# State-space stage of a hybrid backbone: order of subtractions, score rows, gate projections and PSUM banks

## Chip, core and metric

One core of one Trainium2 chip runs the whole program as one launch. The metric is the device time in microseconds (us), the median of several runs. TensorE is called PE here, VectorE DVE, ScalarE ACT, GpSimd POOL.

## What is computed

One layer on 256 context tokens and 512 latent tokens of width 1024: a modulated RMS norm, one input projection, three token mixers (gated linear attention, a 2-D Fourier mix, a bidirectional Mamba-2 state-space mixer), a gated merge, and a top-2 mixture of 16 experts. The change touches the state-space mixer alone, whose reference is, cut short:

```python
def ssd_chunked(x, dt, a, bm, cm, s0):
    '''h_t = exp(dt_t a) h_{t-1} + dt_t x_t B_t^T ; y_t = h_t C_t  (grouped B/C), chunked SSD.'''
    ...
    seg = a_cs[..., :, None] - a_cs[..., None, :]
    decay = jnp.exp(jnp.where(causal, seg, -jnp.inf))
    cb = jnp.einsum('bclgn,bcsgn->bcgls', cm, bm)
    y_diag = jnp.einsum('bcgls,bcgjls,bcsgjp->bclgjp', cb, decay, xdt)
    states = jnp.einsum('bcsgn,bcgjs,bcsgjp->bcgjpn', bm, decay_to_end, xdt)
    ...   # scan over chunks: s = chunk_decay * s + states
    y_off = jnp.einsum('bclgn,bcgjpn,bcgjl->bclgjp', cm, s_prev, jnp.exp(a_cs))
    y = (y_diag + y_off).reshape(B, T, H, P)
```

There are 4 groups of 8 heads of 64 channels, state size 128, and two directions. The result is gated: `rms_norm(y * silu(z)) @ proj`.

## The kernel before

Every engine has its own program, written out by hand in one fixed order, and the engines meet through semaphores only. All work is float32; a float32 matmul over 512 columns stands in the trace as two records. The kernel uses chunks of 128 tokens: 2 of context and 4 latent ones (`TC`, `TL`), taken in the order `ORDER[d]` by direction d.

**The state-space stage** is a loop over the groups g = 0..3. For one group PE does, in this order:

- `project_C` (L441): the C projection; then four x projections `("x", g, m)` (L441 for the latent and L445 for the context tokens, two PSUM banks each) with the transposes of B (L605), the score product CB (L614) and the transposes of x (`x_turn`, L420) between them.
- the z projections in pieces: `z_part(n)` (L629) issues the next n of the group's 32 matmuls, 8 to each of the four z tiles.
- the **first direction's state chain**: `first_state` (L667), then for i = 2..5 `state_step`, which is a state output ("off", four 128-column matmuls, L677) and, up to i = 4, a state part ("kv", one matmul, L684).
- the **loop of the first direction** (d = 0) over pairs of heads b = 0..3: `rows_of` for the next pair (L644 and L646, two matmuls a head, one bank a head, banks 0 and 1), the second direction's `first_state` (b = 0 only) and `state_step(1, b + 2)`, the pair's `y` product (L717, 16 records), and `z_part(2)`. The off and kv products of this direction share bank 2.
- the **loop of the second direction** (d = 1): rows of the next pair, y product of this one, pieces of the next group's B projection (`next_part`, L534; after the last group the first gate projection, L549) and the rows `spread` (L657) for its state outputs.

**The matrices of a head.** Head n of the stage has one of `NM = 4` buffers `mm`. DVE subtracts (`exponents`, L1855: PSUM rows minus a column), ACT takes the exponential (L1387), POOL multiplies by `cb` (L2321), and that allows the y product (`M_ready`). DVE may fill a buffer again once the y product that read it is over (`M_used`), so subtractions run at most two pairs ahead of the y products.

**The state chain.** DVE multiplies the off product out of its bank (L1827) and adds it to yT (L1831); it adds the kv product to the scaled state (L1839; a copy, L1836, for the first). An off product waits until DVE has read the kv before; a kv product waits until DVE has emptied bank 2 of the off product. POOL makes `xw` (L2283), the scaled state (L2303) and `xdt` (L2295). On DVE the second direction's `state_step` and the first direction's `exponents` stand in one hand-written sequence.

**ACT** has `z_silu(3)` (L1364), which needs the fourth z tile complete, between the exponentials of the two directions. Silu and Exp lie in different tables, so each change loads one.

**PSUM banks** are handed out while the program is built: `open_(pe, key, n, lo, hi)` takes the next n banks of the range lo..hi in rotation and makes PE wait until each earlier owner has been read. The x projections, the transposes and CB rotate through all eight banks. DVE's `finish` (L1865, L1872) empties the y banks 4 to 7, and ACT's `raw_evac` (L1286, L1287) empties the banks of B, C and x. Weights come in 2 MB strips through a ring of three slots on the SP queue.

Of the kernel before, what the change touches and what calls it, by code (L numbers as in the profile page):

```python
# [14 lines left out]
P = 128  # L15
D = 1024
T = 512
# [64 lines left out]
def build(nc, a, out):  # L82
    with ExitStack() as ctx:
# [310 lines left out]
        Z_STATES = (3, 3, 2, 2, 2)  # L394

# [15 lines left out]
        def x_turn(pe, g, m, lo=0):  # L411

            pe.wait_ge(S_("xc_ready"), g * 4 + m + 1)
            for half in range(2):
                key = ("xtok", g, m, half)
                ps = open_(pe, key, 1, lo, 8)
# [17 lines left out]
        def _(pe):  # L434
# [155 lines left out]
            for g in range(SG):  # L590
                if g:
                    project_C(g)

                slot = full_strip(pe, w_in, X0 + g * GW)
                for m in range(4):
                    project_T(slot, m, hT, ("x", g, m), nctx=True)
                    strip_used(("x", g, m))
                    if m == 0:
                        pe.wait_ge(S_("BT_ready"), g + 1)
                        for half in range(2):  # L600
                            key = ("Btok", g, half)
                            ps = open_(pe, key)
# [6 lines left out]
                    if m == 1:  # L609
                        pe.wait_ge(S_("CT_ready"), g + 1)  # L610
                        key = ("CB", g)
                        ps = open_(pe, key)
# [4 lines left out]
                    if m >= 1:  # L617
                        x_turn(pe, g, m - 1)
# [17 lines left out]
                x_turn(pe, g, 3, 4)  # L636
# [33 lines left out]
                def state_step(d, i, lo, hi):  # L670
# [9 lines left out]
                    if i < 5:  # L680
                        key = ("kv", g, d, i)
                        pe.wait_ge(S_("xw_ready"), (g * 2 + d) * 5 + i + 1)
                        ps = open_(pe, key, 1, lo, hi)
                        ins = mmul(ps[:, :], Btok[:, t, :], xw[i % 2][:, :], start=True, stop=True)  # L684
                        ins.then_inc(is_full(key)[0], 1)
# [3 lines left out]
                for i in range(2, 6):  # L689
                    for b in range(2):  # L690
                        if g == 0 or i >= 4:
                            spread(g, (i - 2) // 2, (i - 2) % 2 * 2 + b)
                    z_part(Z_STATES[i - 2])
                    state_step(0, i, 4, 8)
                z_part(Z_STATES[4])
                for d in range(2):
                    rows_of(d, 0)
                    rows_of(d, 1)
                    if d:
                        for i in range(2):  # L700
                            next_part(g + 1, i)
                    else:
                        yb = open_(pe, ("y", g), 4, 4, 8)
                    for b in range(HPG // 2):
                        n = (g * 2 + d) * HPG + 2 * b
# [7 lines left out]
                        pe.wait_ge(S_("xdt_ready"), (g * 2 + d) * 4 + b + 1)  # L713
                        pe.wait_ge(S_("M_ready"), n + 2)
                        for c in range(TL):
                            for h in range(2):
                                ins = mmul(yb[h * SHD:(h + 1) * SHD, b * T + c * P:b * T + (c + 1) * P],  # L717
                                           xdt[:, c, (2 * b + h) * SHD:(2 * b + h + 1) * SHD], mm[(n + h) % NM][:, c, :],
                                           start=(d == 0 and c == 0), stop=(d == 1 and c == TL - 1))
                        if d == 0 or b < 3:  # L720
                            ins.then_inc(S_("M_used"), 1)
                        else:
                            ins.then_inc(is_full(("y", g))[0], 1)
                        if d == 0:
                            z_part(2)
                            if b == 3:
                                strip_used(("z", g, 3))
                        else:
# [1734 lines left out]
```

## Time and profile before

| | |
|---|---|
| three runs | 1806.19, 1810.47, 1811.3 us; median 1810.47 us |
| the profiled execution | 1807.78 us, its span 1806.2 us |
| PE busy | 1633.8 us (90%), mean granted clock 0.967 |
| DVE, ACT, POOL busy | 665.0 (37%), 414.6 (23%), 282.8 us (16%) |
| state-space stage | about 90 to 700 us of the span |

A row of the chronological view gives the start, the duration, engine, line, operation, output and inputs, how many records were merged, and in brackets how long the engine stood idle before and which engine and line released it. The duration of a matmul runs to its modelled end, which is later than the start of the next one; the time that a matmul occupies PE is best read from one start to the next.

### The profile page before, as it was taken

The page shows a single profiled execution, that of the slowest core. Times are in us where ns is not written, and L with a number is a line of the kernel's source. Part 1 is how long each engine was busy: PE and PEld are TensorE (multiplying, and loading weights), DVE is VectorE, ACT ScalarE, POOL GpSimd, SP SyncE. Part 2 cuts the span into 40 slices and gives each one's busy share as a digit, 9 for nine tenths or more (in the row PEclk, how much of TensorE's full clock was granted, in tenths as well). Part 3 has the DMA queues.
Part 4 walks back from the last instruction along what each step waited for, and adds up shares of the span by engine and source line. Part 5 has one row for each costly group of instructions (what it writes and reads, how often), then busy time and mean ns, then how long its engine had stood idle before and what let it go on. Part 6 is the DMA issues. An engine that isn't in the chain of part 4 may idle for free. (4 is left out here: it accounts for less than half of the span.)

```text
span 1806.2 us, 23273 instructions
## 1 busy us (share of the span) xinstructions
PE 1633.8 (90%) x9106; PEld 875.3 (48%) x9107; DVE 665.0 (37%) x1086; ACT 414.6 (23%) x771; POOL 282.8 (16%) x311
## 2 busy tenths in 40 slices
PE   5998889899799899999999999999999949999893
PEld 2464454455455444444545555444656525555451
DVE  2544444354363455400126674214025122222224
ACT  4333423243242230000123324210120111111112
POOL 0006404503512530000000000000000022222122
PEclk9999999999999999999999999999989969999997
DMA  9810101101111056312110111123532467998994
GB/s 346 309 47 1 47 24 47 47 24 47 47 47 47 18 210 252 118 55 95 47 46 1 47 47 47 51 89 110 186 140 72 161 256 261 386 346 293 393 380 157
DMA packets 106754, 241.24 MB, mean 134 GB/s; under 512 B 5481, under 2 KB 15214, under 8 KB 106690
## 3 DMA queue, kind: packets, MB, share of 16 engines
q1 hardware_dynamic: 86800, 180.60, 27.8%
q0 software_dynamic: 14288, 48.96, 7.5%
q10 hardware_dynamic: 5602, 10.78, 1.6%
q8 instruction: 45, 0.74, 0.2%
q14 instruction: 19, 0.16, 0.0%
HBM read 218.31 MB, written 22.02 MB: 133 GB/s over the span
## 5 line engine op out<-in xcount | busy, mean ns | idle before, releaser
L441 PE MATMUL psum<-arena 128*128 128x512 f32 x688 | 303.5, 597 | 10.6 <-ACT arena L1287 5.7
L441 PEld LDWEIGHTS psum<-arena 128*128 128x128 f32 x688 | 129.0, 190 | 168.8 <-issue 162.9
L1083 PE MATMUL psum<-arena 128*32 128x256 f32 x2816 | 165.6, 387 | 1.5 <-DVE arena L2205 1.5
L455 PE MATMUL psum<-arena 128*128 128x512 f32 x352 | 155.5, 602 | 1.6 <-issue 1.6
L629 PE MATMUL psum<-arena 128*128 128x512 f32 x256 | 125.4, 626 | 1.0 <-ACT arena L1327 1.0
L1083 PEld LDWEIGHTS psum<-arena 128*32 128x32 f32 x2816 | 92.4, 111 | 59.7 <-issue 7.5
L772 PE MATMUL psum<-arena 128*128 128x512 f32 x256 | 111.5, 593 | 0.0
L455 PEld LDWEIGHTS psum<-arena 128*128 128x128 f32 x352 | 67.5, 194 | 84.0 <-issue 83.7
L2321 POOL TENSOR_TENSOR arena<-arena 128x512 f32<-128x512 f32 x64 | 85.9, 1353 | 98.2 <-ACT arena L1387 98.2
L1747 DVE SCALAR_TENSOR_TENSOR arena<-arena 128x772 f32<-128x772 f32 (+1 forms) x96 | 93.9, 978 | 3.4
L2283 POOL TENSOR_TENSOR arena<-arena 128x512 f32<-128x512 f32 x40 | 41.3, 1040 | 285.7 <-ACT arena L1327 280.7
L1105 PE MATMUL psum<-arena 128*32 128x256 f32 x1408 | 85.1, 382 | 1.0 <-DVE arena L2216 1.0
L2363 POOL DMA_DIRECT2D slots<-arena x92 | 50.1, 546 | 207.2 <-DVE arena L2216 179.7
L2337 POOL IOTA arena<- 128x4 int32 x1 | 0.1, 131 | 516.5 <-DVEq L408 516.5
L772 PEld LDWEIGHTS psum<-arena 128*128 128x128 f32 x256 | 47.9, 189 | 58.8 <-issue 58.8
L2210 DVE TENSOR_TENSOR arena<-arena,psum 128x128 f32<-128x128 f32 x44 | 12.7, 289 | 166.7 <-ACT arena L1587 166.7
L629 PEld LDWEIGHTS psum<-arena 128*128 128x128 f32 x256 | 47.2, 197 | 54.2 <-issue 54.2
L445 PE MATMUL psum<-arena 128*128 128x256 f32 x320 | 72.3, 378 | 0.0
L1855 DVE TENSOR_TENSOR arena<-psum,arena 128x512 f32<-128x512 f32 x64 | 42.6, 688 | 74.1 <-PE psum L646 73.0
L445 PEld LDWEIGHTS psum<-arena 128*128 128x128 f32 x320 | 60.4, 189 | 17.2 <-issue 9.6
L1387 ACT ACTIVATE arena<-arena 128x512 f32<-128x512 f32 x64 | 39.2, 629 | 109.7 <-DVE arena L1855 108.8
L717 PE MATMUL psum<-arena 128*64 128x128 f32 x512 | 38.8, 296 | 27.7 <-POOL arena L2321 27.7
(366 smaller groups left out, 2131.0 us busy)
## 6 DMA issues: line engine op xcount, KB each, us to landing
arena<-exp_w_d SPq DMA_DIRECT2D x48, 2048.0 KB, 17.4
arena<-w_in_d SPq DMA_DIRECT2D x22, 2048.0 KB, 8.0
arena<-ada_w_d POOLq DMA_DIRECT2D x8, 2048.0 KB, 10.4
slots<-arena POOLq DMA_DIRECT2D x1, 9216.0 KB, 27.0
arena<-ada_w_d SPq DMA_DIRECT2D x4, 2048.0 KB, 21.4
arena<-ssd_proj_d SPq DMA_DIRECT2D x4, 2048.0 KB, 11.3
slots<-arena POOLq DMA_DIRECT2D x92, 64.0 KB, 4.9
arena<-slots POOLq DMA_DIRECT2D x22, 256.0 KB, 6.0
```

The source lines that it names most:

```text
L441: ins = mmul(ps[:, 0:T], slot[:, k, m * P:(m + 1) * P], src[:, k, C:NT], start=(k == 0), stop=(k == KD - 1))
L445: ins = mmul(ps[:, T:T + C], slot[:, k, m * P:(m + 1) * P], src[:, k, 0:C], start=(k == 0), stop=(k == KD - 1))
L455: ins = mmul(ps[:, 0:n], src[:, k, t * P:(t + 1) * P], slot[:, k, 0:n], start=(k == 0), stop=(k == KD - 1))
L629: ins = mmul(bank(key)[:, :], slot[:, k, m * P:(m + 1) * P], hT[:, k, C:NT], start=(k == 0), stop=(k == KD - 1))
L772: ins = mmul(pss[m][:, :], slot[:, k, m * P:(m + 1) * P], yT[:, kh * KD + k, :], start=(kh == 0 and k == 0), stop=(kh == 1 and k == KD - 1))
L1083: ins = mmul(psU[q * R:(q + 1) * R, 0:2 * HF], XT[:, k % 2, k // 2, :], w13[p][:, :, k, q * HF:(q + 1) * HF], start=(k == 0), stop=(k == K ...
L1105: ins = mmul(psD[q * R:(q + 1) * R, 0:DQ], heT[:, k, :], w2[:, k, q * DQ:(q + 1) * DQ], start=(k == 0), stop=(k == NQ - 1))
L1747: ins = v.scalar_tensor_tensor(cacc[:, lo:hi], src[:, lo + k:hi + k], w[:, blk * SK + k:blk * SK + k + 1], cacc[:, lo:hi], ALU.mult, ALU.add)
L1855: v.tensor_tensor(mm[n % NM], bank(key)[:, :].rearrange("p (c l) -> p c l", c=TL), acs[:, TC:TT, at:at + 1].to_broadcast([P, TL, P]), ALU. ...
L2283: g_.tensor_tensor(heads(xw[i % 2]), heads(xtok[:, t, :]), wend[:, t, hs:hs + HPG].unsqueeze(2).to_broadcast([P, HPG, SHD]), ALU.mult).the ...
L2321: g_.tensor_tensor(mm[n % NM], mm[n % NM], cb, ALU.mult).then_inc(S_("M_ready"), 1)
L2363: pool.dma_start(rows(b)[:, q * DQ:(q + 1) * DQ].rearrange("(i r) c -> r i c", i=BATCH), half(ysb, b)[q * R:(q + 1) * R, :].rearrange("r ( ...
```

## The change

No operation is added or taken away. Four things change:

1. On DVE the first direction's `exponents` come in pairs: two of them, then one state step of the second direction. The first two subtractions of the second direction stand ahead of `state_step(1, 5)`.
2. On PE `rows_of` in the first loop still stands one pair ahead, and the last turn now issues the second direction's first pair (before, that came after the loop).
3. On PE the z matmuls of that loop leave their place behind the y product. One stands between `first_state` and the first off product, and 2, 2, 2 and 1 stand behind the off products, ahead of kv. POOL's `xw`, scaling and `xdt` are ordered by pairs to match.
4. From group 1 on, the x projections, the transposes and CB get fixed banks (`GROUP_BANKS`); group 0 keeps the rotation.

```diff
+        Z_BEHIND = (2, 2, 2, 1)
+        one = lambda *banks: tuple((b, b + 1) for b in banks)
+        ANY = (0, 8)
+        FIRST_BANKS = ([ANY] * 4, [(ANY, ANY)] * 3, (ANY, ANY), ANY)
+        GROUP_BANKS = (((4, 6), (6, 8), (3, 5), (5, 7)), (one(1, 2), one(7, 2), one(0, 1)), one(2, 3), (0, 1))
...
+                x_at, turn_at, btok_at, cb_at = GROUP_BANKS if g else FIRST_BANKS
...
-                    project_T(slot, m, hT, ("x", g, m), nctx=True)
+                    project_T(slot, m, hT, ("x", g, m), True, *x_at[m])
...
-                for d in range(2):
-                    rows_of(d, 0)
-                    rows_of(d, 1)
-                    if d:
-                        for i in range(2):
-                            next_part(g + 1, i)
...
-                    for b in range(HPG // 2):
-                        if b < 3:
-                            rows_of(d, 2 * b + 2)
-                            rows_of(d, 2 * b + 3)
-                        if d == 0:
-                            if b == 0:
-                                first_state(1, 2, 3)
-                            state_step(1, b + 2, 2, 3)
...
-                        if d == 0:
-                            z_part(2)
...
+                rows_of(0, 0)
+                rows_of(0, 1)
+                yb = open_(pe, ("y", g), 4, 4, 8)
...
+                for b in range(HPG // 2):
+                    for h in range(2):
+                        rows_of((b + 1) // 4, (2 * b + 2 + h) % HPG)
+                    if b == 0:
+                        first_state(1, 2, 3)
+                        z_part(1)
+                    state_off(1, b + 2, 2, 3)
+                    z_part(Z_BEHIND[b])
+                    if b < 3:
+                        state_kv(1, b + 2, 2, 3)
+                    else:
+                        strip_used(("z", g, 3))
+                    y_part(0, b)
+                for i in range(2):
+                    next_part(g + 1, i)
+                for b in range(HPG // 2):
+                    if b < 3:
+                        rows_of(1, 2 * b + 2)
+                        rows_of(1, 2 * b + 3)
+                    y_part(1, b)
...
@@ DVE
-                for i in range(1, 4):
-                    state_step(1, i)
-                    exponents(0, i + 1)
-                exponents(0, 5)
-                state_step(1, 4)
-                exponents(0, 6)
-                state_step(1, 5)
-                exponents(0, 7)
-                for h in range(4):
-                    exponents(1, h)
+                state_step(1, 1)
+                for i in range(2, 5):
+                    exponents(0, 2 * i - 2)
+                    exponents(0, 2 * i - 1)
+                    state_step(1, i)
+                exponents(1, 0)
+                exponents(1, 1)
+                state_step(1, 5)
+                exponents(1, 2)
+                exponents(1, 3)
@@ POOL
-                        if d == 0 and h in (1, 2, 4):
+                        if d == 0 and h in (1, 3, 5):
                             make_xw(1, 2 + h // 2)
-                        if d == 0 and h in (1, 3, 4):
                             scale_state(1, 2 + h // 2)
                         if d == 0 and h in (3, 5, 7):
                             make_xdt(1, h // 2 - 1)
-                        if d == 1 and h == 0:
+                        if d == 1 and h == 1:
                             make_xdt(1, 3)
```

How this moves the instructions, at three places. On **PE, the third and fourth turn of the first direction's loop in group 0**, before (L644 and L646 rows of a head, L677 off, L684 kv, L717 y, L629 z, L534 the next B):

```order
L646 MATMUL psum<-arena 128x512
L677 MATMUL psum<-arena 128x128 x4
L684 MATMUL psum<-arena 128x512
L717 MATMUL psum<-arena 64x128 x8
L629 MATMUL psum<-arena 128x512 x2
L677 MATMUL psum<-arena 128x128 x4
L717 MATMUL psum<-arena 64x128 x8
L629 MATMUL psum<-arena 128x512 x2
L644 MATMUL psum<-arena 128x512
```

and changed (L652 and L654 rows, L685 off, L694 kv, L719 y, L637 z, L541 the next B):

```order
L654 MATMUL psum<-arena 128x512
L685 MATMUL psum<-arena 128x128 x4
L637 MATMUL psum<-arena 128x512 x2
L694 MATMUL psum<-arena 128x512
L719 MATMUL psum<-arena 64x128 x8
L652 MATMUL psum<-arena 128x512
L654 MATMUL psum<-arena 128x512
L652 MATMUL psum<-arena 128x512
L654 MATMUL psum<-arena 128x512
L685 MATMUL psum<-arena 128x128 x4
L637 MATMUL psum<-arena 128x512
L719 MATMUL psum<-arena 64x128 x8
```

The z matmuls moved from behind y to between off and kv, and four row matmuls of the second direction stand in the last turn.

On **DVE, from the second direction's third state step on, group 1**, before (L1855 one subtraction, L1827 and L1831 the off product, L1839 kv):

```order
L1855 TENSOR_TENSOR arena<-psum,arena 128x512 x2
L1827 TENSOR_TENSOR arena<-psum,arena 128x512
L1831 TENSOR_TENSOR arena<-arena 128x4x128
L1839 TENSOR_TENSOR arena<-arena,psum 128x512
L1855 TENSOR_TENSOR arena<-psum,arena 128x512
L1827 TENSOR_TENSOR arena<-psum,arena 128x512
L1831 TENSOR_TENSOR arena<-arena 128x4x128
L1855 TENSOR_TENSOR arena<-psum,arena 128x512 x7
```

and changed (L1873 one subtraction, L1845 and L1849 off, L1857 kv):

```order
L1873 TENSOR_TENSOR arena<-psum,arena 128x512 x2
L1845 TENSOR_TENSOR arena<-psum,arena 128x512
L1849 TENSOR_TENSOR arena<-arena 128x4x128
L1857 TENSOR_TENSOR arena<-arena,psum 128x512
L1873 TENSOR_TENSOR arena<-psum,arena 128x512 x2
L1845 TENSOR_TENSOR arena<-psum,arena 128x512
L1849 TENSOR_TENSOR arena<-arena 128x4x128
L1873 TENSOR_TENSOR arena<-psum,arena 128x512 x4
```

Head 7's subtraction stood behind the last state step of the second direction; now heads 6 and 7 stand together ahead of the last but one, and the second direction's first two ahead of the last.

On **POOL, the products with `cb` of the first direction, group 1**, changed (L2339 a product, L2301 `xw`, L2321 the scaled state, L2313 `xdt`):

```order
L2339 TENSOR_TENSOR arena<-arena 128x512 x2
L2301 TENSOR_TENSOR arena<-arena 128x512
L2321 TENSOR_TENSOR arena<-arena 128x512
L2339 TENSOR_TENSOR arena<-arena 128x512 x2
L2301 TENSOR_TENSOR arena<-arena 128x512
L2321 TENSOR_TENSOR arena<-arena 128x512
L2313 TENSOR_TENSOR arena<-arena 128x4x128
L2339 TENSOR_TENSOR arena<-arena 128x512 x2
L2301 TENSOR_TENSOR arena<-arena 128x512
```

Two products now always stand together; before, other operations stood between the products of heads 2 and 3 and of heads 4 and 5.

## Rows read from the trace of the kernel before

**Rows 1.** PE's waits by line and releaser, 90 to 700 us: total us, times, longest

```profile
PE psum L717 <- POOL arena L2321: 27.7, 17, 4.3
PE psum L684 <- DVE arena L1827: 10.5, 12, 0.9
PE psum L441 <- ACT arena L1287: 5.7, 1, 5.7
PE psum L677 <- DVE arena L1836: 3.5, 4, 0.9
PE psum L644 <- DVE arena L1855: 2.4, 4, 0.6
...
PE psum L629 <- ACT arena L1327: 1.0, 1, 1.0
```

**Rows 2.** By stretch, groups 0 to 3: us, busy us by engine, clock, DMA share, GB/s

```profile
160.12:201.28 41.16, 31.55 (x156) 16.20 (x154) 17.76 (x25) 11.75 (x17) 23.43 (x20) 0.96 0.13 44
309.18:351.20 42.02, 32.42 (x156) 16.81 (x154) 17.77 (x25) 11.75 (x17) 23.42 (x20) 0.92 0.13 43
450.77:491.89 41.12, 31.52 (x155) 16.46 (x154) 17.78 (x25) 11.75 (x17) 23.43 (x20) 0.96 0.13 44
592.67:634.59 41.92, 30.61 (x151) 16.05 (x150) 17.79 (x25) 12.33 (x17) 23.56 (x21) 0.92 0.12 42
```

**Rows 3.** Chronological view, PE, group 1's first-direction loop: start us, duration us

```profile
302.35 1.05 PE L677 MATMUL psum<-arena 128*128 128x128 f32 x8
303.24 1.02 PE L684 MATMUL psum<-arena 128*128 128x512 f32 x2
...
316.45 1.10 PE L684 MATMUL psum<-arena 128*128 128x512 f32 x2 [0.88 <-DVE arena L1827]
317.48 1.10 PE L717 MATMUL psum<-arena 128*64 128x128 f32 x16
318.51 1.99 PE L629 MATMUL psum<-arena 128*128 128x512 f32 x4
320.33 0.38 PE L644 MATMUL psum<-arena 96*128 96x512 bf16 x1
...
321.21 1.05 PE L677 MATMUL psum<-arena 128*128 128x128 f32 x8
...
339.36 1.98 PE L717 MATMUL psum<-arena 128*64 128x128 f32 x16 [4.33 <-POOL arena L2321]
341.27 3.63 PE L629 MATMUL psum<-arena 128*128 128x512 f32 x4
```

**Rows 4.** The same view, DVE, same loop

```profile
329.71 1.81 DVE L1831 TENSOR_TENSOR arena<-arena 128x512 f32<-128x512 f32 x1
...
336.52 0.69 DVE L1855 TENSOR_TENSOR arena<-psum,arena 128x512 f32<-128x512 f32 x1
```

**Rows 5.** The same view, POOL, same loop

```profile
316.51 1.72 POOL L2321 TENSOR_TENSOR arena<-arena 128x512 f32<-128x512 f32 x1
318.19 1.04 POOL L2283 TENSOR_TENSOR arena<-arena 128x512 f32<-128x512 f32 x1
...
337.95 1.26 POOL L2321 TENSOR_TENSOR arena<-arena 128x512 f32<-128x512 f32 x1 [2.97 <-ACT arena L1387]
```

**Rows 6.** The same view, ACT, between the two directions

```profile
344.93 0.60 ACT L1364 ACTIVATE arena<-psum 128x512 f32<-128x512 f32 x1 [5.76 <-PE psum L629]
345.55 1.28 ACT L1387 ACT_TABLE_LOAD   x1
```

**Rows 7.** The same view, PE, from group 0 to group 1

```profile
217.74 7.13 PE L441 MATMUL psum<-arena 128*128 128x512 f32 x16
230.58 9.49 PE L441 MATMUL psum<-arena 128*128 128x512 f32 x16 [5.71 <-ACT arena L1287]
```

**Rows 8.** The same view, DVE, from group 0 to group 1

```profile
217.63 0.69 DVE L1865 TENSOR_TENSOR arena<-arena,psum 128x512 f32<-128x512 f32 x1 [0.74 <-PE psum L717]
```

**Rows 9.** The same view, PE, group 3's second direction

```profile
634.59 1.87 PE L717 MATMUL psum<-arena 128*64 128x128 f32 x16 [2.69 <-POOL arena L2321]
```

More of the change, by code:

```diff
@@ L415, in x_turn @@
                 key = ("xtok", g, m, half)
-                ps = open_(pe, key, 1, lo, 8)
+                ps = open_(pe, key, 1, *at[half])
                 for t in range(3):
@@ L601, in _ @@
                             key = ("Btok", g, half)
-                            ps = open_(pe, key)
+                            ps = open_(pe, key, 1, *btok_at[half])
                             for t in range(3):
@@ L611, in _ @@
                         key = ("CB", g)
-                        ps = open_(pe, key)
+                        ps = open_(pe, key, 1, *cb_at)
                         for c in range(TL):
@@ L635, in _ @@
                 z_part(Z_FRONT)
-                x_turn(pe, g, 3, 4)
+                x_turn(pe, g, 3, ((4, 8), (4, 8)))
                 pe.wait_ge(*is_free(("Btok", g, 1)))
@@ L679, in state_step, with state_kv @@
                     ins.then_inc(is_full(key)[0], 1)
[L680 to L685, printed above, removed]
+                def state_kv(d, i, lo, hi):
+                    key = ("kv", g, d, i)
+                    pe.wait_ge(S_("xw_ready"), (g * 2 + d) * 5 + i + 1)
+                    ps = open_(pe, key, 1, lo, hi)
+                    mmul(ps[:, :], Btok[:, ORDER[d][i], :], xw[i % 2][:, :], start=True, stop=True)\
+                        .then_inc(is_full(key)[0], 1)
                 z_part(2)
@@ L693, in _ @@
                     z_part(Z_STATES[i - 2])
[L694 removed]
+                    state_off(0, i, 4, 8)
+                    if i < 5:
+                        state_kv(0, i, 4, 8)
                 z_part(Z_STATES[4])
[L696 to L732 removed]
@@ new lines, in _, with y_part @@
+                rows_of(0, 0)
+                rows_of(0, 1)
+                yb = open_(pe, ("y", g), 4, 4, 8)
+                def y_part(d, b):
+                    n = (g * 2 + d) * HPG + 2 * b
+                    pe.wait_ge(S_("xdt_ready"), (g * 2 + d) * 4 + b + 1)
+                    pe.wait_ge(S_("M_ready"), n + 2)
+                    for c in range(TL):
+                        for h in range(2):
+                            ins = mmul(yb[h * SHD:(h + 1) * SHD, b * T + c * P:b * T + (c + 1) * P],
+                                       xdt[:, c, (2 * b + h) * SHD:(2 * b + h + 1) * SHD], mm[(n + h) % NM][:, c, :],
+                                       start=(d == 0 and c == 0), stop=(d == 1 and c == TL - 1))
+                    if d == 0 or b < 3:
+                        ins.then_inc(S_("M_used"), 1)
+                    else:
+                        ins.then_inc(is_full(("y", g))[0], 1)
@@ new lines, in _ @@
+                for b in range(HPG // 2):
+                    for h in range(2):
+                        rows_of((b + 1) // 4, (2 * b + 2 + h) % HPG)
[9 more added lines that the diff above has]
+                    y_part(0, b)
@@ L733, in _ @@
+                for i in range(2):
[5 more added lines that the diff above has]
+                    y_part(1, b)
+                    for i in range(2 * b + 2, min(2 * b + 4, 7)):
+                        next_part(g + 1, i)
+                    if g < SG - 1:
+                        spread(g + 1, 0, b)
             open_(pe, ("mod2",), 1, 7, 8)
```

10 lines of the change are left out of this document (3 added, 7 removed).

## Prediction

> **What bounds the kernel now.** The change touches one stage, so I read PE's waits there first [rows 1]. PE is the engine that nearly never stops, and what it waits for in this stage adds up to over 50 us. Half of it is one item: the y product waits 27.7 us in total for POOL's product L2321, 17 times, the longest 4.3 us. Next come 10.5 us in 12 equal waits of the kv product for DVE's L1827, one single wait of 5.7 us of an x projection, four waits of 0.9 us for the state copy L1836, four of 0.6 us for a subtraction, and 1.0 us once for ACT's L1327.
>
> Then the four stretches from a group's first row matmul to the first y product of the second direction [rows 2]. Each lasts 41 to 42 us, PE is busy for about 31, DVE for 18, ACT for 12, POOL for 23. No engine is full: the stretch is bound by latency, by who waits for whom. The clock column says more: 0.92 to 0.96, so part of PE's busy time is at the lower level.
>
> The chronological view shows where [rows 3]. The last y product of the first direction stands idle for 4.33 us, and after that the same 16 records take 1.98 instead of 1.10 us and the z matmuls 3.63 instead of 1.99: half speed, 1.2 instead of 2.4 GHz. Who is late? POOL's product starts at 337.95 after ACT, ACT after DVE's subtraction at 336.52 [rows 4, 5]. That subtraction is head 7's, and in DVE's order it stands behind the second direction's last state step, which needs the off product that PE issues only in this turn. So PE issues the off product, and the y product right behind it must wait for a chain DVE, ACT, POOL that begins with the off product. That is the 4.33 us, once in each of four groups. Afterwards ACT needs Silu on the fourth z tile (0.60 us), whose matmuls stand behind this late y product, and a table load (1.28 us), before it can take the second direction's first exponentials [rows 6]; this gives another wait for POOL at the end of each stretch.
>
> **The change, part by part.** I count PE's work in one stretch from start to start, which is the time a step takes from PE, at full clock [rows 3]: one pair of heads' rows 0.88 us (320.33 to 321.21), off 0.89 (302.35 to 303.24), kv with the change to y 1.03 (316.45 to 317.48), y 1.03 (317.48 to 318.51), two z matmuls 1.82 (318.51 to 320.33). The stretch holds six pairs of rows (5.3), `first_state` as two kv (1.8), four off (3.6), three kv (3.1), four y (4.1), eight z (7.3) and four full B matmuls at a kv's 0.88 (3.5): 28.7 us. No part of the change alters this sum.
>
> *z between off and kv.* It covers the time in which DVE empties bank 2 (0.69 us and the way there and back) with 1.8 us of matmuls. The 12 waits of 0.88 us go, and one z matmul of 0.9 us covers the copy behind `first_state` all but 0.1 us. What z covered so far was the way to the next y product. That cover is needed only if the matrices come late, and this is what the pairs are for.
>
> *Subtractions in pairs.* I walk through the new order, t = 0 at the stretch's start. PE: first rows, the 0.6 us wait for the bank stays, second rows until 2.5; `first_state` to 4.3; z, off, two z, kv to 9.0; y(0) to 10.0. A turn is now 0.9 + 0.9 + 1.8 + 1.0 + 1.0 = 5.7 us: y(1) ends at 15.7, y(2) at 21.4. The last turn has rows, off and one z: y(3) starts at 24.1. The other engines: DVE subtracts heads 4 and 5 at 10.7, as soon as y(0) has freed their buffers and the rows are there, ACT follows within 1.4 us, POOL's two products need 2.5 us. POOL must do `xw`, the scaling and an `xdt` in each turn besides: 2 x 1.26 + 3 x 1.04 = 5.6 us [rows 5], just under PE's 5.7. In this order POOL ends the products of heads 4 and 5 at 15.4 (needed at 20.4) and those of heads 6 and 7 at 21.1 (needed at 24.1). Nothing waits for M before the last y product, and 3.0 us are to spare there. The 4.33 us go, and with them the half clock.
>
> *The second direction's start.* Its rows and subtractions are now early. What is late next is Silu: the fourth z tile is full at 24.1; Silu, the table, two exponentials and two products give 0.6 + 1.3 + 0.7 + 2.6 and hand-overs, 29.4. PE has y(3), the B matmuls and one pair of rows and arrives at 29.6. So the wait is gone where four B matmuls stand there (groups 0 to 2). In group 3 only two gate matmuls stand there, PE arrives at 27.9 and waits 1.6 us: 29.5.
>
> Sum of the stretches: 41.16 + 42.02 + 41.12 + 41.92 = 166.2 us before [rows 2], 3 x 29.6 + 29.5 = 118.3 after: **47.9 us**. In group 3 there is a second wait of 2.69 us, inside the stretch, and the y product behind it takes 1.87 instead of 1.10 us [rows 9]; with the projection that follows I put 1.6 us for the slow clock there.
>
> *Fixed banks.* The 5.7 us wait stands at the passage from group 0 to 1: the rotation gave the first x projection bank 1, in which the C projection lies that PE has just made, and ACT empties it only after B's convolution. x starts at 230.58 instead of 224.6 (217.74 and eight times 0.86), and its eight matmuls take 9.49 instead of 7.13 us [rows 7]: **8.3 us**. With the fixed banks it lies in 4 and 5, whose owner is y. DVE's last read of y starts at 217.63 and takes 0.69 us [rows 8], 6.3 us before x needs the bank. The 1.0 us wait of a z product for ACT's L1327 is a wait for a bank too (group 3); its new owner is an older transpose. **1.0 us**.
>
> What stays: about 1 us in each group at the last y product (what is left of the 27.7 us) and the 0.6 us above. The later stages wait for nothing that has a time of its own; all start from this stage's end, so they move as a whole.
>
> Does faster work collide? A DVE sum of two SBUF operands takes 1.81 us where another operation of this size takes 0.69, and a POOL product 1.72 instead of 1.26, where the two run together [rows 4, 5]. By the largest of each, POOL's products cost 8 x 0.46 = 3.7 us more in a stretch; 3.0 are to spare, so 0.7 us a group would show. I take none in the sum, since most products in these rows stand at 1.26. The Trainium skill says why the two meet (GPSIMD Engine Reference, Key points: the engine shares its SBUF interfaces with VectorE, with contention when VectorE reads two SBUF inputs). By that rule packing POOL fuller makes it slower, and the sum would be that of the first rival; the trace agrees as far as these two rows go.
>
> Total: 47.9 + 1.6 + 8.3 + 1.0 = 58.8 us. Against the profiled execution's 1807.8 us this gives 1749.0. Its time is 2.7 us under the median of the three runs, so for a median I say **1750**.
>
> **The rivals.**
> - *POOL becomes the bound of the first loop.* If all its operations stretch by 1.72 / 1.26, a turn takes 7.6 us against PE's 5.7. Over three turns 6 us are lost, 3 of them are spare: 3 us a group, 12 in all, 1762. For it: POOL is busy without a gap from 3 to 21 in my walk. Against: 23 us busy in 42 now, with few long ones. At the middle of the way it costs 6 us, 1756. Chance 0.12.
> - *The fixed banks move the wait instead of removing it*, to a transpose or a z product that now meets a younger owner. Then 8.3 us stay or stand in three passages at 2 to 3 us each: 1758. Against: each new owner that I followed is read microseconds before. Chance 0.05.
> - *The change does not do what it says.* If DVE still gets to heads 6 and 7 late, because a subtraction waits for a y product that waits for POOL, the 4.33 us and the slow clock stay (4 x 6.4 us): 1776. The order of the instructions speaks against it. Chance 0.03.
> - *Slower.* From group 1 on x always needs banks 4 to 7, which y holds until DVE's last step. If that step came later than the 6.3 us after y's end, PE would stand, with the clock loss of [rows 7] (2.4 us) on top. Only if it came some 26 us late would three passages at 22 us eat the gain and more: 1815. DVE has 18 of 42 us to do here, and its step follows y within 1 us. Chance 0.02.
>
> **How the numbers follow.** The forecast has 0.78. Its own bounds: the steps are read to 0.1 us, 16 turns, and the remaining waits of a few us, 1743 to 1756. The range must take in the first two rivals to their upper prices: 1743 to 1763. A measurement of this kernel tells 0.3% (5.4 us) from no change. Faster by more 0.97, within it 0.01, slower 0.02.
>
> **What would show it.** PE's waits for POOL fall from 27.7 us to 4 to 7, with no wait over 2 us. The waits of kv for DVE and the 5.7 us are gone. The four stretches last 29 to 30 us at clock 1.00. Wrong would be: a y product in the first loop that waits for POOL (POOL as the bound), a new wait behind an x projection (banks), or a stretch of the later stages that grew.

## The result, and the profile after

The changed kernel takes 1741.41 us, the median of 4 runs (1738.72 to 1744.89), against 1809.85 us before: ratio 0.962, 95% interval 0.961 to 0.964. Faster was forecast, 1750 us with a range from 1743 to 1763: the gain is 68 us where 60 were forecast, and the time lies 1.6 us below the range. The profiled execution took 1743.69 us (span 1742.1), 64.1 us less than the one profiled before.

The page of the changed kernel, PE's busy time and the granted clock in 40 slices:

```profile
PE 1613.3 (93%) x9106; PEld 865.1 (50%) x9107; DVE 663.0 (38%) x1086; ACT 414.4 (24%) x771; POOL 284.2 (16%) x311
...
PEclk9999999999999999999999999999999969999997
```

and the same clock line of the kernel before:

```profile
PEclk9999999999999999999999999999989969999997
```

PE is busy for 1613 us, 20 us less than before with the same work. Most of that is time at half clock that is gone: by the mean granted clock PE lost 59.6 us of its span to the lower level before (0.033 of 1806.2) and 43.6 now (0.025 of 1742.1), 16 us less. The page's 40 slices are too coarse to show where: both lines stand at 9 all through this stage, though [rows 2] has 0.92 to 0.96 there. The short stretches below show it.

PE's waits by line and releaser from 90 to 700 us (total, times, longest), to be laid beside [rows 1]:

```profile
PE psum L719 <- POOL arena L2339: 5.4, 6, 1.5
PE psum L652 <- DVE arena L1873: 2.4, 4, 0.6
PE psum L675 <- POOL arena L2301: 1.4, 4, 0.4
PE psum L652 <- ACT arena L1391: 0.9, 6, 0.2
PE psum L448 <- DVE arena L1883: 0.8, 1, 0.8
PE psum L685 <- DVE arena L1857: 0.6, 1, 0.6
```

L719 is the y product: 5.4 us in 6 waits instead of 27.7 in 17. The 12 waits of kv, the copy's four, the 5.7 us at the x projection and the 1.0 us of a z product are not there. The row waits (L652) are those of before.

The four stretches from the first row matmul of a group to the second direction's first y product, by stretch, to be laid beside [rows 2]:

```profile
161.51:190.70 29.19, 28.56 (x155) 15.16 (x154) 15.89 (x24) 11.03 (x15) 23.14 (x20) 1.00 0.15 51
290.27:319.45 29.18, 28.56 (x155) 15.16 (x154) 15.94 (x24) 11.02 (x15) 23.13 (x20) 1.00 0.15 51
419.00:448.21 29.21, 28.59 (x156) 15.16 (x154) 16.86 (x24) 11.03 (x15) 23.06 (x20) 1.00 0.15 51
547.78:576.78 29.00, 26.91 (x151) 14.43 (x150) 16.95 (x25) 12.12 (x17) 22.96 (x20) 1.00 0.15 49
```

29.2, 29.2, 29.2 and 29.0 us instead of 41.2, 42.0, 41.1 and 41.9, all at clock 1.00. PE is busy for 28.6 of them.

Group 1's loop on PE in the chronological view (L652 a row, L685 off, L637 z, L694 kv, L719 y, L541 the next group's B), to be laid beside [rows 3]:

```profile
300.21 0.39 PE L652 MATMUL psum<-arena 96*128 96x512 bf16 x1
...
301.10 1.05 PE L685 MATMUL psum<-arena 128*128 128x128 f32 x8
301.99 1.88 PE L637 MATMUL psum<-arena 128*128 128x512 f32 x4
303.71 1.02 PE L694 MATMUL psum<-arena 128*128 128x512 f32 x2
304.66 1.10 PE L719 MATMUL psum<-arena 128*64 128x128 f32 x16
305.70 0.39 PE L652 MATMUL psum<-arena 96*128 96x512 bf16 x1
...
313.91 1.10 PE L719 MATMUL psum<-arena 128*64 128x128 f32 x16
314.94 3.70 PE L541 MATMUL psum<-arena 128*128 128x512 f32 x8
...
319.45 1.10 PE L719 MATMUL psum<-arena 128*64 128x128 f32 x16
```

No bracket stands in these rows: none of these instructions waited. A turn takes 5.49 us (300.21 to 305.70). The last y product of the direction (313.91) and the first of the next (319.45) come when PE gets to them; before, the first of these two stood idle for 4.33 us. POOL in the same loop (L2339 products, L2313 `xdt`):

```profile
303.53 2.95 POOL L2339 TENSOR_TENSOR arena<-arena 128x512 f32<-128x512 f32 x2
...
308.45 1.55 POOL L2313 TENSOR_TENSOR arena<-arena 128x512 f32<-128x512 f32 x1
309.96 2.50 POOL L2339 TENSOR_TENSOR arena<-arena 128x512 f32<-128x512 f32 x2
```

The products of heads 6 and 7 end at 312.5, the y product needs them at 313.9: 1.5 us to spare, not 3.0. A pair of products takes 2.95 us and one `xdt` 1.55 where DVE's sum of two SBUF operands (L1849) stands beside them, and 2.50 and 1.04 elsewhere in this loop:

```profile
302.92 1.20 DVE L1849 TENSOR_TENSOR arena<-arena 128x512 f32<-128x512 f32 x1
...
308.40 0.69 DVE L1849 TENSOR_TENSOR arena<-arena 128x512 f32<-128x512 f32 x1
```

The passage from group 0 to 1 (C projection and x projection merged into one row), beside [rows 7]:

```profile
207.16 14.00 PE L448 MATMUL psum<-arena 128*128 128x512 f32 x32
```

16 matmuls (32 records) in 14.0 us without a wait, 0.87 us each, the pace of the first row of [rows 7].

**Where the 64 us came from.** Cut at the first row matmul and at the first matmul behind the state-space stage (both starts from the chronological view):

| | up to the first row | state-space loop | later stages |
|---|---|---|---|
| before | 160.1 | 489.8 | 1156.2 |
| changed | 161.5 | 429.0 | 1151.6 |
| difference | +1.4 | -60.8 | -4.7 |

The stage gave 60.8 us where 58.8 were forecast. The later stages, which the change does not touch in the code, gave 4.7 us where nothing was. The experiments are about both. The 1.4 us lost ahead of the first row are clock: from 30 us of the span to the first row PE does the same work, and is busy for 126.2 us at a mean granted clock of 0.95 instead of 124.6 at 0.96. Why was not tested.

### The profile page after: what moved, and what is told of

Read it like the earlier page. It is cut to its first block and busy times, and to the rows that moved or that the text cites. A ratio compares the mean times of both kernels' runs of the same rounds, so it can differ in the third digit from the quotient of the medians.

```text
span 1742.1 us, 23271 instructions
## 1 busy us (share of the span) xinstructions
PE 1613.3 (93%) x9106; PEld 865.1 (50%) x9107; DVE 663.0 (38%) x1086; ACT 414.4 (24%) x771; POOL 284.2 (16%) x311
## 5 line engine op out<-in xcount | busy, mean ns | idle before, releaser
L448 PE MATMUL psum<-arena 128*128 128x512 f32 x688 | 300.9, 593 | 3.6 <-DVEq L415 2.8
L448 PEld LDWEIGHTS psum<-arena 128*128 128x128 f32 x688 | 128.1, 189 | 160.1 <-issue 154.2
L462 PE MATMUL psum<-arena 128*128 128x512 f32 x352 | 154.1, 597 | 0.0
L1101 PEld LDWEIGHTS psum<-arena 128*32 128x32 f32 x2816 | 91.9, 111 | 60.8 <-issue 7.9
L637 PE MATMUL psum<-arena 128*128 128x512 f32 x256 | 118.8, 596 | 0.0
L790 PE MATMUL psum<-arena 128*128 128x512 f32 x256 | 111.5, 593 | 0.0
L2339 POOL TENSOR_TENSOR arena<-arena 128x512 f32<-128x512 f32 x64 | 87.6, 1389 | 45.4 <-ACT arena L1405 45.4
L2301 POOL TENSOR_TENSOR arena<-arena 128x512 f32<-128x512 f32 x40 | 41.3, 1040 | 277.8 <-ACT arena L1345 272.8
L790 PEld LDWEIGHTS psum<-arena 128*128 128x128 f32 x256 | 47.9, 189 | 58.8 <-issue 58.8
L637 PEld LDWEIGHTS psum<-arena 128*128 128x128 f32 x256 | 45.4, 189 | 47.4 <-issue 47.4
L1873 DVE TENSOR_TENSOR arena<-psum,arena 128x512 f32<-128x512 f32 x64 | 41.8, 688 | 52.9 <-PE psum L654 52.4
L837 PE MATMUL psum<-arena 128*128 128x512 f32 x128 | 61.1, 595 | 0.0
L905 PE MATMUL psum<-arena 128*128 128x512 f32 x128 | 57.0, 607 | 2.1 <-ACT arena L1507 2.1
```

What stands on the lines that cost most here:

```text
L448: ins = mmul(ps[:, 0:T], slot[:, k, m * P:(m + 1) * P], src[:, k, C:NT], start=(k == 0), stop=(k == KD - 1))
L462: ins = mmul(ps[:, 0:n], src[:, k, t * P:(t + 1) * P], slot[:, k, 0:n], start=(k == 0), stop=(k == KD - 1))
L637: ins = mmul(bank(key)[:, :], slot[:, k, m * P:(m + 1) * P], hT[:, k, C:NT], start=(k == 0), stop=(k == KD - 1))
L790: ins = mmul(pss[m][:, :], slot[:, k, m * P:(m + 1) * P], yT[:, kh * KD + k, :], start=(kh == 0 and k == 0), stop=(kh == 1 and k == KD - 1))
L837: ins = mmul(bank(key)[:, :], slot[:, k, key[1] % 4 * P:(key[1] % 4 + 1) * P], hT[:, k, C:NT], start=(k == 0), stop=(k == KD - 1))
L905: ins = mmul(ps[:, :], slot[:, k, m * P:(m + 1) * P], src[:, k, :], start=(k == 0), stop=(k == KD - 1))
```

## The experiments

For every kernel the same two lengths are given, "stage" and "later", from its one trace; the times are medians of several runs. The kernel before was run again beside each set. Theory A is my forecast's: a part is worth the waits it removes and the slow clock behind them.

### Each part alone or left out

**Fixed banks alone**, in the kernel before, from group 1 on; `x_turn`, `Btok` and `CB` get theirs likewise:

```diff
-                    project_T(slot, m, hT, ("x", g, m), nctx=True)
+                    project_T(slot, m, hT, ("x", g, m), True, *x_at[m])
...
```

> The kernel before with the fixed banks alone, all orders as before. Theory A (each part is worth the waits it removes): the 5.7 us wait of the first x projection of group 1, the slow clock behind it (2.4 us) and the 1.0 us z wait go, everything else stays: 9 us faster than before, about 1801, with the y products' 27.7 us of waits for POOL unchanged. Rival B (the parts need each other; the wait only moves while the loop is slow): 0 to 3 us faster, with a new wait behind an x projection or a transpose. Rival C (the later stages gained because the state-space stage ends earlier): a part of the later stages' gain shows here too, from the end of this stage on over 2 us.

Measured: 1792.6 us against 1809.4, ratio 0.992 (0.990 to 0.995). Stage 480.5 (-9.4), later 1149.7 (-6.6). PE's waits from 90 to 700 us:

```profile
PE psum L723 <- POOL arena L2327: 27.6, 17, 4.3
PE psum L690 <- DVE arena L1833: 10.5, 12, 0.9
```

The y products wait 27.6 us as before, the x projection does not wait. For the stage theory A holds to 0.4 us, and B falls. But the kernel is 17 us faster, not 9: the rest lies in the later stages. C had the place right; the reason is another, as the rotation below shows.

**The changed kernel without fixed banks:**

```diff
-                x_at, turn_at, btok_at, cb_at = GROUP_BANKS if g else FIRST_BANKS
+                x_at, turn_at, btok_at, cb_at = FIRST_BANKS
```

> The changed kernel with the rotation of banks as before. Theory A: 9 us slower than the changed kernel, about 1750, by one wait of 5 to 6 us at the first x projection of group 1 with a stretch of half clock behind it. Rival B: within 2 us of the changed kernel, since the C projection's bank is emptied in time when the group ends earlier.

Measured: 1755.2 us (1748.9 to 1760.8), ratio to before 0.970 (0.967 to 0.972). Stage 438.5, 9.5 more than the changed kernel; later 1159.4, 7.8 more.

```profile
PE psum L448 <- ACT arena L1305: 5.7, 1, 5.7
PE psum L719 <- POOL arena L2339: 5.4, 6, 1.5
...
PE psum L637 <- ACT arena L1345: 1.0, 1, 1.0
```

The 5.7 and the 1.0 us are back to the digit. B falls: ending the group earlier doesn't help, since C's bank is late relative to C. In all it is 14 us slower than the changed kernel where 9 were expected; the stage gives the 9.5, the rest stands in the later stages. The six times stand in two groups, three from 1748.9 to 1750.7 at a mean clock of 0.975 to 0.977 and three from 1759.8 to 1760.8 at 0.970 or 0.971: the same program, 10 us (0.6%) apart, as its clocks are. The trace, and with it the 1159.4, is of the slowest of the six.

**z between off and kv alone**, in the kernel before (`state_step` takes the number of z matmuls to issue behind its off product):

```diff
                                 first_state(1, 2, 3)
+                                z_part(1)
-                            state_step(1, b + 2, 2, 3)
+                            state_step(1, b + 2, 2, 3, (2, 2, 2, 1)[b])
...
-                        if d == 0:
-                            z_part(2)
```

> The kernel before with the z products between off and kv alone (1, then 2, 2, 2, 1), subtractions and rows as before. Theory A: the 12 waits of kv and most of the 4 for the state copy go (13 us, 17 with the hand-over), the wait at the last y product falls by one z matmul to about 3.4 us, the 1 us wait at the second direction's first y goes since Silu comes earlier, and a new wait of about 1 us stands at the third y: some 20 to 28 us faster than before, about 1786. Rival B (without the pairs the z products are missed behind y, and the waits for POOL grow by what kv no longer waits): under 10 us faster, over 1800, with the waits for POOL above 35 us.

Measured: 1784.9 us against 1809.4, ratio 0.987 (0.985 to 0.989). Stage 467.9 (-21.9), later 1156.6, as before.

```profile
PE psum L721 <- POOL arena L2321: 23.2, 15, 3.5
PE psum L441 <- ACT arena L1287: 5.7, 1, 5.7
PE psum L644 <- DVE arena L1855: 4.6, 8, 0.6
```

A holds: 24.5 us faster, and kv no longer waits. The y products' waits fall only from 27.7 to 23.2, the longest is 3.5 (one z matmul stands ahead of it now), and the x projection's wait is untouched. The rows' waits for DVE grow from 2.4 to 4.6 us, which was not expected.

**The pairs without z**: the changed kernel with z behind y:

```diff
                         first_state(1, 2, 3)
-                        z_part(1)
                     state_off(1, b + 2, 2, 3)
-                    z_part(Z_BEHIND[b])
...
                     y_part(0, b)
+                    z_part(2)
```

> The changed kernel with the z products behind y as before, pairs of subtractions, rows and banks kept. Theory A: the kv waits come back (12 of 0.88 us and 4 for the copy, 17 us with hand-over), the last y product of the first direction waits for nothing, and the second direction's first y waits about 1 us again (2.7 in group 3) because Silu is later: 22 us slower than the changed kernel, about 1763. Rival B (the gain is the z products' alone): over 1780, with waits of 4 us at the last y product.

Measured: 1766.5 us where 1763 were expected, ratio to before 0.976 (0.974 to 0.978), 25 us slower than the changed kernel. Stage 451.3, 22.3 more than 429.0, where 22 were expected.

```profile
PE psum L694 <- DVE arena L1844: 10.5, 12, 0.9
PE psum L719 <- POOL arena L2338: 5.7, 6, 1.7
PE psum L685 <- DVE arena L1853: 3.5, 4, 0.9
...
PE psum L541 <- ACT arena L1381: 2.3, 3, 0.8
```

The waits of kv (L694) and of the off product behind the copy (L685) are back as they were, and the y products (L719) still wait for 5.7 us only: it is the pairs that remove the 4.33 us. By difference the pairs (subtractions, rows and POOL's order together) are worth some 29 us of the stage: 489.8 - 451.3 - 9.4 = 29.1 here, and 467.9 - 438.5 = 29.4 on top of z. So in the stage the three parts add up: 29.1 + 22.3 + 9.4 = 60.8. No run has the pairs alone, nor one of their three reorderings without the others. A new wait stands at the next B projection (L541), for Silu to empty z's bank: the late z tile that I had named as the next thing late.

### What happened in the later stages

**Both kernels again, unchanged.**

> The kernel before, unchanged, for a second trace and more times. Theory D (the later stages' share of the gain is where the half-clock stretches happen to fall): the state-space stage again lasts 489.8 us from its first row matmul to its last product, the later stages anything from 1149 to 1160 us, along with their half-clock time. Rival C (the later stages gained because of the change): the later stages again last 1156 us within 1 us.

> The changed kernel, unchanged. Theory D: the state-space stage again 429.0 us, the later stages anything from 1149 to 1160 us, single times from 1738 to 1750. Rival C: the later stages again 1151.6 us within 1 us, all times within 3 us.

Measured: before 1810.4 us (ratio 1.000, 0.999 to 1.001), changed 1742.7 us (0.963, 0.962 to 0.964). Stage 491.3 and 429.0, later 1156.9 and 1150.8. The later stages of before, second trace, in one stretch, and then those of the changed kernel, first trace (columns as in [rows 2]):

```profile
650.73:1807.60 1156.87, 1064.08 (x6742) 564.11 (x6742) 377.90 (x690) 192.65 (x400) 92.14 (x143) 0.97 0.45 165
```

```profile
590.51:1742.10 1151.59, 1060.09 (x6742) 561.61 (x6742) 377.79 (x690) 192.61 (x400) 92.11 (x143) 0.97 0.45 165
```

The later lengths repeat: 1156.2 and 1156.9 against 1151.6 and 1150.8. That speaks against D, pure chance, but two traces of each are few, since one unchanged program above gave times 10 us apart. (The stage of before took 1.5 us more in its second trace, 491.3 against 489.8.) What in the change could do it? Of its parts only the banks reach there: fixed banks alone shorten the later stages, z alone does not. `open_` keeps one rotation over banks 0 to 7 for the whole program. The fixed banks take part in it no longer, and so it stands at bank 0 at the stage's end instead of bank 4, and every later product lies in another bank. In before, the first k projection (848 us) falls on the bank pair of the first decay product, which DVE (L1927) is still reading. A second wait, at 1388 us (L455), has no releaser that the profile shows. The two, of before:

```profile
PE psum L455 <- issue: 1.6, 1, 1.6
...
PE psum L441 <- DVE arena L1927: 1.3, 1, 1.3
```

In the changed kernel neither is there. That gives a test with one number:

```diff
+            nxt[(0, 8)] = 0
             open_(pe, ("mod2",), 1, 7, 8)
```

in the kernel before, and the opposite (`= 4`) in the changed one.

> The kernel before with one number changed: behind the state-space stage the rotation over banks 0 to 7 goes on at bank 0, where the changed kernel leaves it, instead of bank 4. Theory F (the fixed banks also shift the rotation of all later stages, and the later stages' share of the gain comes from that): the 1.3 us wait of the first k projection for DVE goes, the half-clock stretches behind it fall elsewhere, the later stages last 1150 to 1153 us instead of 1156 to 1157, the state-space stage stays at 489.8: about 1804. Theory D (chance): no change against before beyond 1.3 us, 1809.

> The changed kernel with the rotation set back to bank 4 behind the stage, as before. Theory F: state-space stage 429.0 us as in the changed kernel, the 1.3 us wait of the k projection back, later stages 1156 to 1159 us: about 1748. Theory D: within 2 us of the changed kernel, 1742 to 1744.

Measured: before with the rotation from bank 0: 1802.7 us against 1810.1, ratio 0.997 (0.995 to 0.998); stage 489.9 as before, later 1150.1:

```profile
649.84:1799.90 1150.06, 1060.09 (x6742) 562.37 (x6742) 378.09 (x690) 192.69 (x400) 91.92 (x143) 0.97 0.46 165
```

Changed with the rotation from bank 4: 1744.1 us, ratio to before 0.964 (0.963 to 0.966). Both waits are back:

```profile
PE psum L462 <- issue: 1.6, 1, 1.6
...
PE psum L448 <- DVE arena L1946: 1.3, 1, 1.3
```

but the later stages take 1151.9, not 1156 or more:

```profile
590.67:1742.60 1151.93, 1057.70 (x6742) 560.95 (x6742) 377.70 (x690) 192.75 (x400) 92.50 (x143) 0.97 0.46 165
```

Half right. One number, no instruction moved, makes the kernel before 7.4 us faster; 2.9 of it are the two waits. The rest goes with the clock: for the same 6742 records PE is busy for 1060.1 us behind the stage and not 1064.1. In the changed kernel the two waits come back and the half-clock time does not; PE is busy for 1057.7 us there, less than in any other trace. I expected 1748 and got 1744, only 1.4 us over the changed kernel's 1742.7. So one and the same step of the rotation is worth 7.4 us in one kernel and 1.4 in the other; only the two waits follow it in both.

What the clock does is easily seen at one place, the Fourier mixer's small matmuls. PE waits for nothing there, in either kernel. A stretch of before, then one of the changed kernel in the same part of the program (it holds more of the work, 52 records against 31):

```profile
1327.60:1338.00 10.40, 10.40 (x31) 5.73 (x31) 2.43 (x1) 1.70 (x4) 0.00 (x0) 0.51 1.03 396
```

```profile
1268.00:1279.00 11.00, 11.00 (x52) 7.09 (x52) 2.49 (x1) 3.72 (x8) 0.00 (x0) 1.00 1.03 397
```

Clock 0.51 for 10 us against 1.00. From the first slow matmul of before (1327.64) to the first of the next line (1339.94) are 12.30 us; the same matmuls take 7.59 in the changed kernel (1268.58 to 1276.17). It is tempting to see in these 4.7 us the 4.7 us of the later stages. The trace of before with the rotation from bank 0 says no. One row of this part, in before, in the changed kernel, and in that one:

```profile
1334.90 5.20 PE L960 MATMUL psum<-arena 128*128 128x257 f32 x16
```

```profile
1272.60 3.74 PE L978 MATMUL psum<-arena 128*128 128x257 f32 x16
```

```profile
1332.44 6.34 PE L961 MATMUL psum<-arena 128*128 128x257 f32 x16
```

It runs at half clock here too, and its later stages are short all the same. The changed kernel with the rotation from bank 4 has 3.74 us in this row, as the changed kernel has. So this slow stretch does not follow the rotation: the half-clock time of the later stages lies at several places, and the sum alone, PE's busy time, can be compared.

Over the traces with the rotation at bank 0 (changed twice, fixed banks alone, z behind y, before with `= 0`, and the two with more POOL work, below) the later stages last 1149.7 to 1153.0 us, mean 1151.0; with the rotation at bank 4 (before twice, no banks, z alone, changed with `= 4`) 1151.9 to 1159.4, mean 1156.2. That is 5.2 us on average, 2.9 of them waits. These are single traces of unlike kernels, the 1159.4 among them; what shows that the rotation matters are the medians of before with and without `= 0`.

**Does any shift do it?** Two more 512-column matmuls behind the stage, in each kernel:

```diff
+            for _ in range(2):
+                mmul(ps[:, :], ones, ssum, start=True, stop=True)
             mmul(ps[:, :], ones, ssum, start=True, stop=True).then_inc(is_full(key)[0], 1)
```

> The kernel before with two more matmuls of 512 columns (1.7 us) behind the state-space stage, into a bank that the next one overwrites. Theory D: 1.7 us slower than before, with the same spread. Rival E (the place of the later stages in time decides, so any shift of the end changes them): the median moves by 4 us or more in either direction, with another half-clock time in the later stages.

> The changed kernel with the same two more matmuls (1.7 us). Theory D: 1.7 us slower than the changed kernel, about 1743, same spread. Rival E: the median moves by 4 us or more, towards 1747 to 1750.

Measured: 1813.8 us (1803.2 to 1815.3, ratio 1.001) and 1746.3 us (0.964), against 1810.7 and the changed kernel's 1742.7; later 1160.2 and 1154.4. Both grew by 3 to 4 us for 1.7 us of work, less than E's 4 and more than D's 1.7. A shift costs or gives some us by the clock, but it does not turn one kernel's later stages into the other's. Inconclusive between the two.

### How much room POOL has

The scaling of the second direction's state once more in the first kernel and twice more in the second (`range(2 if d else 0)`), same values, each with a wait for the one before:

```diff
+                    for _ in range(1 if d else 0):
+                        more[0] += 1
+                        g_.tensor_tensor(heads(Send), heads(S[(i - 1) % 2]),
+                                         eend[:, ORDER[d][i], hs:hs + HPG].unsqueeze(2).to_broadcast([P, HPG, SHD]),
+                                         ALU.mult).then_inc(S_("more"), 1)
+                        pool.wait_ge(S_("more"), more[0])
```

> The changed kernel with one more scaling of the state (about 1.1 us, the same values written) on POOL in each of the three turns that have one, second direction only: 3.3 us more POOL work ahead of the last two products of the first direction. My walk left 3.0 us to spare there: 0 to 0.5 us a group slower, within 2 us of the changed kernel. If POOL were already the bound of the loop: 3.3 us a group, 13 us slower.

> The same with two more scalings in each turn, 6.6 us of POOL work a group. By the walk 3.6 us of it show at the last y product of the first direction in each group, 14 us in all, and more where that wait brings half clock: 1757 to 1765. If the room on POOL is larger than worked out, a smaller part: under 1750.

Measured: 1750.7 us (1747.3 to 1755.2, ratio 0.969), stage 435.5, 6.5 more than 429.0; and 1763.7 us (ratio 0.975), stage 449.2, 20.2 more. With three more, PE's waits in all groups, and then the two in group 1's loop:

```profile
PE psum L719 <- POOL arena L2346: 7.3, 10, 0.9
...
PE psum L694 <- POOL arena L2302: 2.2, 4, 0.7
```

```profile
310.51 1.13 PE L694 MATMUL psum<-arena 128*128 128x512 f32 x2 [0.69 <-POOL arena L2302]
...
316.18 1.10 PE L719 MATMUL psum<-arena 128*64 128x128 f32 x16 [0.65 <-POOL arena L2346]
```

kv (L694) waits 0.69 us for `xw` in groups 1 to 3 (0.16 in group 0), and the last y product 0.65 us for the products in each group. With six more:

```profile
PE psum L685 <- DVE arena L1857: 10.3, 9, 1.4
PE psum L719 <- POOL arena L2346: 7.3, 10, 1.0
PE psum L694 <- POOL arena L2302: 4.6, 4, 1.2
```

The second was expected, 14 us and more. The first was not: 1.6 us a group where 0 to 0.5 were said. The spare is the 1.5 us of the view above, and `xw` has little more (it ends at 307.5 in the changed kernel, kv begins at 309.2). My 3.0 us shrank from both ends: POOL ends the products of heads 6 and 7 22.2 us after the stretch's start, not 21.1, since it lost 1.4 us to slower operations, and PE gets there after 23.6 us, not 24.1. POOL is not the bound of the changed kernel, but it is 1.5 us from being it.

## Why the prediction was right and wrong

- **The bound.** Right: latency by who waits for whom, and the chain off, DVE, ACT, POOL ahead of the last y product. The pairs take this wait away with z still behind y; z alone leaves 3.5 of it.
- **z between off and kv.** Right: all 12 waits of kv and the copy's four are gone; taking z back costs 22.3 us of stage, 22 expected.
- **The stretches.** 118.3 us forecast, 116.6 measured. Mis-sized: kv with the change to y was read as 1.03 us from a row that itself followed a wait; without one it is 0.95 (303.71 to 304.66). Two z matmuls, read as 1.82 us with rows behind them, take 1.72 with kv behind them (301.99 to 303.71). So a turn is 5.49 and not 5.65 us. The second direction's start was right: no wait in groups 0 to 2, in group 3 1.5 us where 1.6 were said. The 1.6 us for the slow clock behind group 3's wait came as said: from the second direction's first y product to the stage's end 15.4 us before (634.59 to 649.96), 13.7 now (576.78 to 590.51).
- **Half clock in the stage.** Right: all gone, 1.00 in the four stretches.
- **The fixed banks in the stage.** 9.3 us forecast (8.3 and 1.0); alone they gave 9.4, left out they cost 9.5.
- **The step that failed** is the sentence "The later stages wait for nothing that has a time of its own; all start from this stage's end, so they move as a whole." They don't: cut by stages, they took 4.7 us less in the profiled pair. The fixed banks leave the rotation at another bank, and with it two waits of 1.3 and 1.6 us far behind the stage go; this is shown in both kernels. The 1.3 us wait could be read before: it stands in the trace with its releaser, and the rotation is in `open_`. Besides, PE is busy for 4.1 us less there (1064.2 and 1060.1 us, the same 6742 records), which is less time at half clock, and the waits for the experts' weights (`exp_w_d`) are 2.0 us longer in this trace of the changed kernel (7.5 against 5.5; 5.6 in its second). Why the half-clock time is less stays open: setting the rotation gives 7.4 us in the kernel before, but only 1.4 in the changed one.
- **The range.** From the forecast of 1750 to the measured 1741.4 are 8.6 us: 2.0 of the stage, 4.7 of the later stages, less the 1.4 at the start; 1.0 that I had added to the 1749.0 of the sum; and 2.3 by which the profiled execution lies above the median of its four runs. The range's lower end was the stage's sum with reading errors alone, as if the rest of the program had none. Without the later stages' 4.7 us the time would lie inside it. The rest is luck either way: the changed kernel's nine runs have a median of 1742.7 us and go from 1738.7 (mean clock 0.978) to 1744.9 (0.974), five below 1743 and four above.
- **POOL as a rival** did not come true, though its room was half of what I gave it. The page of the Trainium skill that I cited for it (GPSIMD Engine Reference, Key points) pointed the right way: a pair of products took 2.95 instead of 2.50 us where DVE's sum of two SBUF operands stood beside it. The size in this loop was 1.4 us, against the 3.7 that I had worked out from the largest rows.
- **Slower and the moved wait** did not come true: no x projection, transpose or z product waits for a bank in the changed stage.

## What to carry to other kernels

When one engine's fixed order makes it serve chain A late because chain B's step stands ahead of it, look for the step that begins only when the waiting engine has moved on, and pair the steps so that a whole pair is ahead. Cover a short bank hand-over with work that has no successor in a hurry, but first make sure that what this work covered so far is no longer late. And a rotation of banks is state that runs through the whole program: whoever takes owners out of it in one stage should list the waits of all later stages, and look for the start of the rotation that gives the fewest.

## What the runs showed that I had not expected

- One number that shifts the bank rotation (no instruction added, removed or moved) made the kernel before 7.4 us faster, 0.3% (interval 0.2 to 0.5%).
- PE fell to the lower of its two clock levels, 1.2 GHz (granted clock 0.51 over 10.4 us), in the Fourier mixer with no wait before or in it, in a part with many matmuls on few partitions or of 129 and 258 columns; in the changed kernel the same part ran at 1.00. It stayed at 1.00 with the rotation set back to bank 4, and it was slow in before at either bank. What decides it the traces don't say, and it was not tried.
- The same program without fixed banks gave times 10 us apart, with mean clocks of 0.970 and 0.977. A difference under 10 us in this kernel needs traces of both sides, cut by stage: the stage's length repeated to 0.1 us in the changed kernel (429.0 in four traces: twice unchanged, shifted, and with the rotation at bank 4) and to 1.5 us in before (489.8 to 491.3), while the changed kernel's times alone moved by 6.

What stays open: why the changed kernel with the rotation set back keeps its short later stages, and so how much of the gain behind the stage, beyond the 2.9 us of the two waits, comes from the rotation at all. Not tried: an earlier fourth z tile for group 3's 1.5 us, and another filling for the 1 us at the last y product of each group; together they are some 5 us of waits.
